# Moving activations, whole weight slabs and block sums to another distance, modulo 512 bytes, from the weight ring

## The chip, the cores and the metric

The kernel runs on one core of one Trainium2 chip. The metric is the device time of one execution in microseconds (us); lower is better. One execution is also recorded by the hardware profiler, and all rows below are of that one. TensorE is called PE in the rows, its weight loads PEld, VectorE DVE, ScalarE ACT and GpSimd POOL. SP issues most of the transfers from memory.

## The reference

One decoder layer, 512 tokens by 2048 channels, all in float32. Cut to what matters:

```
proj = x @ w_in                      # 2048 -> 4180, split among four head groups
mix  = concat(pool(..), conv(..), sparse_attention(..), nsa_attention(..))
x    = layernorm(alpha * x + mix @ w_out)             # 2048 -> 2048
gate, up = split(x @ w_gate_up)                       # 2048 -> 2 * 5632
x    = layernorm(alpha * x + (silu(gate) * up) @ w_down)   # 5632 -> 2048
```

The three large matrix products (w_in, w_out, and the feed-forward pair w_gate_up and w_down) hold most of the work, the feed-forward part by far the most.

## The kernel before

**Every product is three matmuls.** A float32 operand is split into a high part (rounded to the format float32r) and a low part (what is left). A product is high times high, high times low and low times high, each a matmul instruction of its own with its own load of 128 weight columns: the *stationary* operand is loaded into the array, the *moving* operand streams past it. L799 to L801 are the three in the input projection and in the first slabs of the feed-forward part, L1034 to L1036 those of the output projection, L1152, L1154 and L1156 those of gate and up, L1201, L1203 and L1205 those of down.

**The feed-forward part** uses a seven-product scheme on blocks of 2 by 2 (Strassen's form). A chunk makes 128 columns of gate and up for all 512 tokens by seven products; one product is 8 steps of three matmuls, 24 in all, each with 128 weight columns stationary and 256 tokens moving. There are 42 chunks of this kind. Their seven products, numbered 0 to 6 by the second argument of `product`, take as moving operand:

- products 0, 5 and 6: quarters of `act`, the split activations themselves;
- product 1: the block sum s1, which lies in `xs_1` in the room `x_room`;
- product 2: s2, in `xs_2`, in `x_room` as well;
- product 3: s4, in `xs_4`, a room of its own (in the rows `xs`);
- product 4: s3, which was written over a quarter of `act`.

The weights of all seven come from the *ring*: four places for a high part and four for a low one in `w_room`, each of 1024 words per partition. After every four chunks two units of down follow, with the blocks of the hidden layer (`h`, `hs`) stationary and the ring moving, 512 columns wide.

**Whole slabs** of 2048 words are what the stages ahead of the chunks use: two in `w_room` too, laid over the ring but starting `SHIFT` words later, and for a few slabs at the seam between output projection and feed-forward two in `x_room` (`spare_1`, `spare_2`) and one in `xs_4` (`spare_4`).

**Who feeds PE.** SP loads weights into `raw` and `raw_c`; ACT writes the high part into the ring (L1490), DVE the low part (L2041) and the differences of weight blocks (L2049 to L2056). All of this order is written out by hand, with semaphores; there is no scheduler. PE waits for `lo_ready` ahead of each product.

**Where things lie.** The distances within a partition follow from the sizes in the code. All rooms but a few have sizes that are multiples of 512 bytes, so only the start modulo 512 matters for what is told here. Counted from the start of the ring, modulo 512 bytes:

| room | before | after |
|---|---|---|
| ring in `w_room` (high and low places) | 0 | 0 |
| whole slabs in `w_room` | 32 | 64 |
| `act`, with s3 in it | 32 | 64 |
| `raw` | 32 | 64 |
| s1 in `xs_1` | 64 | 32 |
| s2 in `xs_2`, s4 in `xs_4`, and the slabs `spare_1`, `spare_2`, `spare_4` | 64 | 64 |
| `h` blocks, `hs`, `raw_c`, the last weights (`late`) in `x_room`, the mixers' tiles in `proj` | 0 | 0 |

Of the kernel before, what the change touches and what calls it, by code (L numbers as in the profile page):

```python
# [21 lines left out]
F32 = mybir.dt.float32  # L22
F32R = mybir.dt.float32r
# [4 lines left out]
P = 128  # L28
# [22 lines left out]
SLAB = 2048  # L51
# [47 lines left out]


GRAN = SLAB // 2
SHIFT = 8
X_SHIFT = 144
HALF_TOKS = SEQ // 2
S_ORDER = ("s1", "s2", "s4", "s3")
TAIL_SLOTS = ((0, 32), (2, 32), (4, 63), (5, 63), (1, 32), (3, 32), (0, 33), (2, 33))
# [36 lines left out]
def build(nc, x, x_t, w_in, w_out, pool_w, pool_scale, conv_w, conv_b, conv_ln_g, conv_ln_b, conv_pw_w,  # L143
          conv_pw_b, cmp_pos_k, cmp_pos_v, cmp_k_w1, cmp_k_w2, cmp_v_w1, cmp_v_w2, ln1_g, ln1_b,
          ln2_g, ln2_b, w_gate_up, w_down, out):
    with ExitStack() as ctx:
        def sb(name, shape, dt=F32, where=ctx):
            return where.enter_context(nc.sbuf_tensor(name, shape, dt))

        def sem(name):  # L150
# [5 lines left out]
        std = sb("std", [P, TT])  # L156
        w_room = sb("w_room", [P, 4 * SLAB + P + SHIFT], F32R)
        w_hi, w_lo = (w_room[:, SHIFT + at:SHIFT + at + 2 * SLAB].rearrange("p (s n) -> p s n", s=2)
                      for at in (0, 2 * SLAB + P))
# [3 lines left out]

        between = sb("between", [P, P - SHIFT])

# [30 lines left out]
        feed = ExitStack()  # L196
# [17 lines left out]
        h23 = sb("h23", [P, 2, 2, SEQ], F32R, feed)  # L214
        a2_scope = ExitStack()
        with a2_scope:
            below_s1 = sb("below_s1", [P, X_SHIFT], F32, a2_scope)
            s1 = sb("s1", [P, KT // 2, HALF_TOKS], F32, a2_scope)
            below_a2 = sb("below_a2", [P, SLAB], F32, a2_scope)
            a21 = sb("a21", [P, KT // 2, HALF_TOKS], F32, a2_scope)  # L220
            a22 = sb("a22", [P, KT // 2, HALF_TOKS], F32, a2_scope)
        x_room = sb("x_room", [P, 4 * SLAB + X_SHIFT], F32R, feed)
        xs_1, xs_2 = (x_room[:, X_SHIFT + at:X_SHIFT + at + 2 * SLAB].rearrange("p (a k n) -> p a k n", a=2, n=HALF_TOKS)
                      for at in (0, 2 * SLAB))
        first_norm = ExitStack()
        with first_norm:
            ln1_gain = sb("ln1_gain", [P, D_MODEL], F32, first_norm)
# [2 lines left out]
        with s4_scope:  # L230
# [20 lines left out]


        spare_1, spare_2 = ((x_room[:, at:at + SLAB], x_room[:, at + SLAB:at + 2 * SLAB])
                            for at in (X_SHIFT, X_SHIFT + 2 * SLAB))
        spare_4 = tuple(xs_4[:, a, :, :].rearrange("p k n -> p (k n)") for a in range(2))
        late = [(x_room[:, at:at + GRAN], x_room[:, at + GRAN:at + 2 * GRAN]) for at in range(0, 8 * GRAN, 2 * GRAN)]

# [2003 lines left out]
```

How the kernel before makes its waits and increments, by code:

```python
        def copied(eng, n):  # L451
            eng.wait_ge(bank_free[n % 2], n // 2 + 1)
# [1 line left out]
        def tile_ready(eng, group, slab, i):  # L455
            if i < TT - 1:
                eng.wait_ge(tile_done, group * (TT - 1) + (i + 1))
            else:
                eng.wait_ge(slab_done, slab + 1)
# [4 lines left out]
        @block.sync  # L465
# [19 lines left out]
            rows = ((conv_w[0], 0, CONV_WIDTH), (conv_b, V_CB, 1), (conv_ln_g, V_LG, 1),  # L485
                    (conv_ln_b, V_LB, 1), (conv_pw_b, V_PB, 1), (pool_scale, V_PS, 1))
            for src, at, n in rows:
                nc.sync.dma_start(sel[at:at + n, 0:SEQ], src).then_inc(small_loaded, 16)
            nc.sync.dma_start(sel[0:CMP_BLOCK, SEQ:SEQ + P], cmp_pos_k[0]).then_inc(small_loaded, 16)
            nc.sync.dma_start(sel[CMP_BLOCK:2 * CMP_BLOCK, SEQ:SEQ + P], cmp_pos_v[0]).then_inc(small_loaded, 16)
            nc.sync.dma_start(w2[:, 0, :], cmp_k_w2[0]).then_inc(small_loaded, 16)
            nc.sync.dma_start(w2[:, 1, :], cmp_v_w2[0]).then_inc(small_loaded, 16)
            for n in (2, 3):
                sp.wait_ge(part_lo, n + 3)
                load(n % 2, win[:, :, C_IQ + n * P:C_IQ + (n + 1) * P], KT)
            sp.wait_ge(split_done, N_IKWG - 1)
            ikwg = raw[:, 0, 0:KT * (W_IKW + W_NG)].rearrange("p (k n) -> p k n", k=KT)
# [2 lines left out]
            with sp.Fori(0, 4) as c:
                sp.wait_ge(split_done, 2 * c + (N_CONV - 1))
                load(1, win[:, :, bass.ds(c * P + C_G, P)], KT)
```

## Time and profile before

| | before |
|---|---|
| median of 3 runs | 1964.51 us (1962.86 to 1965.04) |
| the profiled execution | 1964.08 us |
| its span, first to last instruction | 1962.2 us |
| PE busy, of the span | 99% |
| DVE busy, of the span | 72% |
| ACT busy, of the span | 43% |
| chunks and down units together | from 710.5 us to 1905.9 us of the span |

The profiled execution's own time lies 1.9 us above its span. A busy PE says only that some matmul was under way: matmuls overlap each other in the rows, since one takes some 280 ns from its start to its end while the next starts after less than half of that. How fast PE goes is read from the starts, by dividing the time between two of them by the matmuls that start between.

### The profile page before, as it was taken

The page shows a single profiled execution, that of the slowest core. Times are in us where ns is not written, and L with a number is a line of the kernel's source. Part 1 is how long each engine was busy: PE and PEld are TensorE (multiplying, and loading weights), DVE is VectorE, ACT ScalarE, POOL GpSimd, SP SyncE. Part 2 cuts the span into 40 slices and gives each one's busy share as a digit, 9 for nine tenths or more (in the row PEclk, how much of TensorE's full clock was granted, in tenths as well). Part 3 has the DMA queues.
Part 4 walks back from the last instruction along what each step waited for, and adds up shares of the span by engine and source line. Part 5 has one row for each costly group of instructions (what it writes and reads, how often), then busy time and mean ns, then how long its engine had stood idle before and what let it go on. Part 6 is the DMA issues. An engine that isn't in the chain of part 4 may idle for free.

```text
span 1962.2 us, 30226 instructions
## 1 busy us (share of the span) xinstructions
PE 1952.2 (99%) x12301; PEld 1731.7 (88%) x12301; DVE 1412.2 (72%) x1911; ACT 848.4 (43%) x1280; POOL 504.1 (26%) x343
## 2 busy tenths in 40 slices
PE   9999999999999999999999999999999999999998
PEld 7777888866888999998989999899998989999896
DVE  3079997274112988887878888888788888878777
ACT  3011001265000545556565555655555555555553
POOL 2555656244567310202011020201102020110200
PEclk9999999999999999999999999999999999999999
DMA  7433343500524524938557394754839376493972
GB/s 214 105 89 80 92 103 90 177 21 25 214 86 131 170 65 129 184 118 166 136 130 172 114 187 126 156 149 116 186 98 203 111 158 152 111 200 90 204 244 87
DMA packets 316429, 264.28 MB, mean 135 GB/s; under 512 B 12262, under 2 KB 258854, under 8 KB 313482
## 3 DMA queue, kind: packets, MB, share of 16 engines
q1 hardware_dynamic: 292026, 211.97, 37.7%
q0 software_dynamic: 23616, 46.15, 14.1%
q10 hardware_dynamic: 656, 4.33, 0.6%
q8 instruction: 93, 1.52, 0.3%
q14 instruction: 38, 0.31, 0.1%
HBM read 211.95 MB, written 50.33 MB: 134 GB/s over the span
## 4 chain that ended last, share of the span: by engine, by line
PE 96%; DMA 1%; DVE 1%; ACT 1%; issue 0%; SPq 0%; DVEq 0%
PE psum L1152 14%; PE psum L1156 14%; PE psum L1154 14%; PE psum L799 7%; PE psum L801 7%; PE psum L800 7%; PE psum L1201 6%; PE psum L1203 6%; PE psum L1205 6%; PE psum L1034 3%; PE psum L1035 3%; PE psum L1036 3%; PE psum L1013 1%; PE psum L950 1%; PE psum L941 1%; PE psum L1001 1%
## 5 line engine op out<-in xcount | busy, mean ns | idle before, releaser
L2041 DVE TENSOR_TENSOR w_room<-raw,w_room 128x1024 fp32r<-128x1024 f32 x310 | 379.5, 1224 | 158.9 <-ACT w_room L1490 158.8
L1490 ACT CAST w_room<-raw 128x1024 fp32r<-128x1024 f32 x312 | 329.1, 1055 | 211.3 <-DVE raw L2052 70.3
L769 POOL DMA_DIRECT2D out<-stage x160 | 139.5, 1472 | 1017.5 <-DVE stage L2152 996.8
L1152 PE MATMUL psum<-act,w_room 128*128 128x256 f32 x1344 | 375.7, 280 | 0.0
L1154 PE MATMUL psum<-act,w_room 128*128 128x256 f32 x1344 | 375.4, 279 | 0.0
L1156 PE MATMUL psum<-act,w_room 128*128 128x256 f32 x1344 | 375.3, 279 | 0.0
L1152 PEld LDWEIGHTS psum<-act,w_room 128*128 128x128 f32 x1344 | 252.6, 188 | 0.4
L1154 PEld LDWEIGHTS psum<-act,w_room 128*128 128x128 f32 x1344 | 252.6, 188 | 0.4
L1156 PEld LDWEIGHTS psum<-act,w_room 128*128 128x128 f32 x1344 | 252.8, 188 | 0.0
L799 PE MATMUL psum<-act,w_room 128*128 128x512 f32 (+2 forms) x608 | 231.8, 381 | 1.7 <-DVE act L1716 1.2
L800 PE MATMUL psum<-act,w_room 128*128 128x512 f32 (+2 forms) x608 | 230.0, 378 | 0.0
L801 PE MATMUL psum<-act,w_room 128*128 128x512 f32 (+2 forms) x608 | 229.9, 378 | 0.0
L677 POOL TENSOR_TENSOR w_room<-raw,w_room 128x2048 fp32r<-128x2048 f32 (+1 forms) x45 | 207.4, 4609 | 3.8
L1152 PE MATMUL psum<-x_room,w_room 128*128 128x256 f32 x672 | 185.6, 276 | 0.0
L1156 PE MATMUL psum<-x_room,w_room 128*128 128x256 f32 x672 | 185.5, 276 | 0.0
L1154 PE MATMUL psum<-x_room,w_room 128*128 128x256 f32 x672 | 185.5, 276 | 0.0
L2041 DVE TENSOR_TENSOR w_room<-raw_c,w_room 128x1024 fp32r<-128x1024 f32 x124 | 151.6, 1223 | 46.9 <-ACT w_room L1490 45.1
L674 POOL TENSOR_SCALAR w_room<-raw 128x2048 fp32r<-128x2048 f32 (+1 forms) x45 | 88.9, 1975 | 259.5 <-PE psum L801 136.9
L799 PEld LDWEIGHTS psum<-act,w_room 128*128 128x128 f32 (+1 forms) x608 | 113.8, 187 | 26.9 <-issue 4.4
L800 PEld LDWEIGHTS psum<-act,w_room 128*128 128x128 f32 (+1 forms) x608 | 113.8, 187 | 22.1 <-issue 0.5
L801 PEld LDWEIGHTS psum<-act,w_room 128*128 128x128 f32 (+1 forms) x608 | 113.8, 187 | 22.1
L1490 ACT CAST w_room<-raw_c 128x1024 fp32r<-128x1024 f32 x126 | 132.9, 1055 | 0.0
(303 smaller groups left out, 4121.5 us busy)
## 6 DMA issues: line engine op xcount, KB each, us to landing
raw_c<-in_w_gate_up SPq DMA_DIRECT2D x84, 512.0 KB, 6.6
raw<-in_w_gate_up SPq DMA_DIRECT2D x84, 512.0 KB, 5.8
out<-stage POOLq DMA_DIRECT2D x160, 256.0 KB, 8.2
raw<-in_w_in SPq DMA_DIRECT2D x30, 1024.0 KB, 5.8
raw<-in_w_down SPq DMA_DIRECT2D x46, 512.0 KB, 4.8
raw_c<-in_w_down SPq DMA_DIRECT2D x42, 512.0 KB, 4.4
raw<-in_w_out SPq DMA_DIRECT2D x16, 1024.0 KB, 5.1
acc<-in_x SPq DMA_DIRECT2D x1, 4096.0 KB, 12.5
```

What stands on the lines that cost most here:

```text
L677: nc.gpsimd.tensor_tensor(lo, raw[:, slot, 0:words], hi.bitcast(F32), ALU.subtract)\
L769: nc.gpsimd.dma_start(out_dram[:, tile, n * SEQ:(n + 1) * SEQ], part, accum_op=ALU.add)\
L799: nc.tensor.matmul(out_ap, stat_hi, mov_hi, start=first, stop=False)
L800: nc.tensor.matmul(out_ap, stat_hi, mov_lo, start=False, stop=False)
L801: return nc.tensor.matmul(out_ap, stat_lo, mov_hi, start=False, stop=last)
L1152: nc.tensor.matmul(out_ap, stat_hi[:, cols], mov_hi[:, k, :], start=opens and k == 0, stop=False, skip_group_check=not opens)
L1154: nc.tensor.matmul(out_ap, stat_hi[:, cols], mov_lo[:, k, :], start=False, stop=False, skip_group_check=not opens)
L1156: mm = nc.tensor.matmul(out_ap, stat_lo[:, cols], mov_hi[:, k, :], start=False, stop=k == kh - 1, skip_group_check=not opens)
L1201: nc.tensor.matmul(out_ap[:, i, :], room[:, 0, j, toks], w_h[:, cols], start=opens and j == 0, stop=False, skip_group_check=not opens)
L1203: nc.tensor.matmul(out_ap[:, i, :], room[:, 1, j, toks], w_h[:, cols], start=False, stop=False, skip_group_check=not opens)
L1490: nc.scalar.copy(ring_hi(at), src).then_inc(hi_ready, 1)
L2041: nc.vector.tensor_tensor(lo, src, hi.bitcast(F32), ALU.subtract).then_inc(lo_ready, 1)
```

## The change

Two constants are changed, and the places of three things follow. `SHIFT` grows from 8 words (32 bytes) to 16 (64 bytes): the slabs in `w_room` begin that much behind the ring's start, and `w_room` gets 8 words longer, by which `act` and `raw` behind it move up. `between` gets shorter by the same, so that nothing behind it moves. In `x_room` the 144 words below the sums become 8 below s1 and 16 below s2; xs_1 loses its distance of 576 bytes (64 modulo 512) and gets one of 32. `below_s1` and `below_a2`, which nobody reads, keep the source of s1 on top of its low part. The program has the same instructions in the same order on each of the five engines, before and after; only addresses differ.

```diff
-SHIFT = 8
-X_SHIFT = 144
+SHIFT = 16
+S1_SHIFT = 8
...
-            below_s1 = sb("below_s1", [P, X_SHIFT], F32, a2_scope)
+            below_s1 = sb("below_s1", [P, S1_SHIFT], F32, a2_scope)
             s1 = sb("s1", [P, KT // 2, HALF_TOKS], F32, a2_scope)
-            below_a2 = sb("below_a2", [P, SLAB], F32, a2_scope)
+            below_a2 = sb("below_a2", [P, SLAB + SHIFT - S1_SHIFT], F32, a2_scope)
...
-        x_room = sb("x_room", [P, 4 * SLAB + X_SHIFT], F32R, feed)
-        xs_1, xs_2 = (x_room[:, X_SHIFT + at:X_SHIFT + at + 2 * SLAB].rearrange("p (a k n) -> p a k n", a=2, n=HALF_TOKS)
-                      for at in (0, 2 * SLAB))
+        x_room = sb("x_room", [P, 4 * SLAB + SHIFT], F32R, feed)
+        xs_1, xs_2 = (x_room[:, at:at + 2 * SLAB].rearrange("p (a k n) -> p a k n", a=2, n=HALF_TOKS)
+                      for at in (S1_SHIFT, SHIFT + 2 * SLAB))
...
-                            for at in (X_SHIFT, X_SHIFT + 2 * SLAB))
+                            for at in (SHIFT, SHIFT + 2 * SLAB))
```

## Rows read from the trace of the kernel before

**Rows 1.** The page: span, busy time by engine, the end chain.

```profile
span 1962.2 us, 30226 instructions
PE 1952.2 (99%) x12301; PEld 1731.7 (88%) x12301; DVE 1412.2 (72%) x1911; ACT 848.4 (43%) x1280; POOL 504.1 (26%) x343
PE 96%; DMA 1%; DVE 1%; ACT 1%; issue 0%; SPq 0%; DVEq 0%
```

**Rows 2.** Stretches of the run: busy us and instructions of each engine.

```profile
core 0: us, PE busy (x) PEld busy (x) DVE busy (x) ACT busy (x) POOL busy (x), PEclk, DMA share, GB/s
710.00:1906.00 1196.00, 1196.00 (x8741) 1130.19 (x8740) 985.02 (x1113) 673.10 (x914) 142.22 (x166) 1.00 0.62 149
```

**Rows 3.** PE's timeline at three borders between products of one chunk: start, duration.

```profile
810.19 0.28 PE L1152 MATMUL psum<-x_room,w_room 128*128 128x256 f32 x1
...
818.35 0.28 PE L1152 MATMUL psum<-act,w_room 128*128 128x256 f32 x1
...
829.56 0.28 PE L1152 MATMUL psum<-x_room,w_room 128*128 128x256 f32 x1
```

**Rows 4.** One window per product, PE alone: products 0 to 6.

```profile
807.39:810.19 2.80, 2.80 (x25) 1.00 1.15 158
810.19:812.91 2.72, 2.72 (x26) 1.00 1.06 185
812.91:815.64 2.73, 2.73 (x27) 1.00 1.13 204
815.64:818.36 2.72, 2.72 (x27) 1.00 1.11 220
818.36:821.17 2.81, 2.81 (x27) 1.00 1.16 314
821.17:823.97 2.80, 2.80 (x27) 1.00 1.20 292
823.97:826.77 2.80, 2.80 (x27) 1.00 0.41 101
```

**Rows 5.** PE's timeline, 512-column matmuls: starts at the borders of runs.

```profile
624.55 0.40 PE L1034 MATMUL psum<-x_room,act 128*128 128x512 f32 x1
630.15 0.40 PE L1034 MATMUL psum<-w_room,act 128*128 128x512 f32 x1
...
688.00 0.40 PE L799 MATMUL psum<-act,xs 128*128 128x512 f32 x1
699.19 0.39 PE L799 MATMUL psum<-act,w_room 128*128 128x512 f32 x1
710.08 0.62 PE L1142 MATMUL psum<-act 128*128 128x512 f32 x2
```

**Rows 6.** The first chunk and the start of the second, columns as in Rows 2.

```profile
713.34:721.82 8.48, 8.48 (x74) 8.48 (x73) 8.48 (x9) 5.36 (x8) 0.00 (x0) 1.00 0.32 90
721.82:733.34 11.52, 11.52 (x98) 11.52 (x97) 9.88 (x13) 5.56 (x8) 0.00 (x0) 1.00 0.44 119
733.34:741.50 8.16, 8.16 (x74) 8.16 (x73) 6.60 (x11) 5.22 (x9) 0.00 (x0) 1.00 0.53 151
```

**Rows 7.** DVE's timeline: the low part that product 3 of the same chunk waits for.

```profile
810.80 1.22 DVE L2041 TENSOR_TENSOR w_room<-raw_c,w_room 128x1024 fp32r<-128x1024 f32 x1
```

**Rows 8.** Groups by form on DVE and PE: xcount, busy us, mean ns, idle before.

```profile
L2041 DVE TENSOR_TENSOR w_room<-raw,w_room 128x1024 fp32r<-128x1024 f32 x310 | 379.5, 1224 | 158.9 <-ACT w_room L1490 158.8
L2041 DVE TENSOR_TENSOR w_room<-raw_c,w_room 128x1024 fp32r<-128x1024 f32 x124 | 151.6, 1223 | 46.9 <-ACT w_room L1490 45.1
...
L799 PE MATMUL psum<-act,w_room 128*128 128x512 f32 x528 | 207.2, 392 | 1.7 <-DVE act L1716 1.2 <-ACT proj L1316 0.4
L1034 PE MATMUL psum<-w_room,act 128*128 128x512 f32 x224 | 87.7, 392 | 0.0
L1034 PE MATMUL psum<-x_room,act 128*128 128x512 f32 x32 | 12.7, 398 | 0.0
```

## The prediction

> **What bounds the kernel now.** I read the page first. PE is busy in 99% of the span and holds 96% of the chain that ended last; DVE, the next engine, is at 72% [rows 1]. So only what makes PE's matmuls fewer or quicker can move the end, and the change leaves their number and order alone. The second view is the table of windows. The chunks and down units take 1196 us, 61% of the span, with PE busy throughout and DVE in 985 us, or 82% [rows 2]. In that stretch nothing makes PE wait, so its time is the sum of its own matmuls' spacings. A busy PE hides how quick it is, so the third view is PE's timeline, read for starts. At 810.19 product 1 of a chunk begins, at 818.35 product 4, at 829.56 product 1 of the chunk behind [rows 3]. From 810.19 to 818.35 there are products 1, 2 and 3, or 72 matmuls in 8.16 us: 2.72 us a product, 113.3 ns a matmul. From 818.35 to 829.56 there are products 4, 5, 6 and 0, or 96 matmuls in 11.21 us: 2.80 us a product, 116.8 ns a matmul.
>
> The windows, one for each product, show the same [rows 4]: 2.80 (product 0), 2.72, 2.73, 2.72 (1 to 3), 2.81 (4), 2.80, 2.80 (5 and 6), at a granted clock of 1.00 in all. (Their counts are 25 to 27, not 24: up to three matmuls from ahead of a border are still ending behind it.) All seven have one shape, 128 weight columns and 256 tokens, their weights come from the same ring, and no engine is waited for. They differ in where the moving operand lies: at 64 bytes from the ring, modulo 512, for the three at 2.72, at 32 for the four at 2.80. The transfers are no explanation: products 5 and 6 take the same 2.80 us, with a DMA share of 1.20 and of 0.41.
>
> A fourth view says whether place matters elsewhere. Matmuls of 512 columns with slabs outside `w_room` are slower as well [rows 5]. From 624.55 to 630.15 there are two tiles of 12 with a slab of `x_room` (at 64) moving and `act` (at 32) stationary: 5.60 us, or 233.3 ns each. From 688.00 to 699.19 the 48 of a slab with `xs_4` (at 64) stationary and `act` moving take 11.19 us, 233.1 ns each. From 699.19 to 710.08 the 48 with slab and `act` both at 32 take 10.89 us, 226.9 ns each.
>
> I choose to read all this as one thing: the spacing depends on the distance of moving and stationary operand modulo 512. At 512 columns a distance of 0 gives 227 ns and 32 either way 233; at 256 columns 32 gives 116.8 and 64 gives 113.3.
>
> At this point a rule of the Trainium skill stands against the change. "TensorE: Matmul & The Clock Gate" (Part 2, Step-by-step: what each phase is for) says that moving operand and weight load have an SBUF read port each, so that loading the next weights takes nothing from the running matmul. By that rule the distance wouldn't matter and the sum below would be 0, where by the rows it is 11 us. The trace disagrees: 2.72 against 2.80 us for products alike in all but place [rows 4].
>
> **The change part by part.**
>
> *Products 0, 4, 5 and 6 go from 32 to 64.* Four products of 11.21 us together [rows 3] become four of 2.72, or 10.88: 0.33 us less for each chunk. All 42 chunks: 13.9 us less. This is the mean over chunks in the steady state; the first is different (below).
>
> *Product 1 goes from 64 to 32.* From 2.72 to the 2.80 of product 0 [rows 4]: 0.08 us more, for 42 chunks 3.4 us more. No row has `xs_1` at 32, so the bounds are nothing (it stays at 2.72) and 0.09 us (as product 4, 2.81), 0 to 3.8 us. I take 3.4, since products 0, 5 and 6 agree.
>
> *Slabs in the spare rooms.* `act` comes to 64, where `spare_1`, `spare_2` and `spare_4` lie: distance 0 in place of 32. L1034 has 32 matmuls of that form [rows 8], its two sister lines as many: 96, four times the 24 of rows 5, each time 5.60 less 5.44 (half of 10.89), 0.16 us: 0.6 us less. The slab of `xs_4`: 11.19 less 10.89, 0.3 us less. Together 0.9 us.
>
> *Slabs in `w_room` with `act`* (projections, the first slabs of the feed-forward part): both move by 32, distance 0 as before. No change, if it is the distance that counts.
>
> *Down, the tail, attention:* `h`, ring, `late` and `proj` stay. No change.
>
> *DVE and ACT* read `raw` at 64 now. DVE's L2041 takes 1224 ns from `raw` (at 32) and 1223 from `raw_c` (at 0) [rows 8], so place costs it nothing; I take the same for ACT.
>
> *Is there room for a quicker PE?* A chunk would last 0.25 us less of 19.4. The low part for product 3 of the chunk read above is begun at 810.80 and done 1.22 us later, at 812.02 [rows 7]; the product starts at 815.64 [rows 4]: 3.6 us of slack. DVE's 82% would become 83%. The work that hides behind PE stays hidden.
>
> Sum: 13.9 − 3.4 + 0.9 = 11.4 us less. The profiled execution took 1964.08 us, 0.4 below the median of the runs, 1964.51. So 1952.7 for it, and about 1953.1 for a median. With only starts at two decimals the 0.33 is good to some 0.02, or 0.8 us over all chunks: the case's own range is 1950.5 to 1955.
>
> **The rivals.**
>
> *A. Product 1 stays quick,* since what makes `act` slow is something other than distance 32 (its rows are 2048 bytes apart, those of the sums 1024), and place at 64 still helps `act`. Then the 3.4 us don't come: 1949.7. Against it: 512-column matmuls from a slab of `x_room`, packed as tightly as the sums, are slow at a distance of 32.
>
> *B. Place doesn't matter at all;* the 0.08 us belong to the rows of `act` being 2048 bytes apart. Then only noise is left: 1964.5, no change. For it: the quick three are just those not in `act`. Against it: the same rows of `act` as stationary operand take 5.60 us with one slab and 5.44 with another [rows 5]. The rule that the Trainium skill gives in "TensorE: Matmul & The Clock Gate", quoted above, would lead to this case as well.
>
> *C. At 512 columns the place 64 itself is slow,* not the distance. Rows 5 can't exclude it: both groups at 233 ns have one operand at 64. Then the chunks gain 10.5, the spare slabs nothing, but all slabs with `act` become as slow as the spare ones: 528 and 224 matmuls on one line each [rows 8], times three lines, 2256, at 0.16 us for 24: 15.0 us more. Sum +4.5: 1969, slower. Against it: nothing but the down products and the ring, which go at 227 at place 0, as slabs do at 32, so that place alone has shown no effect between these two. It decides from some 1,600 of these matmuls on.
>
> *D. A second rhythm of PE.* In the first chunk products 1 to 3 take 8.48 us (2.83 each) and products 4 to 6 with product 0 of the second 11.52 (2.88 each); from 733.34 products 1 to 3 take 8.16 again [rows 6]. Nobody is waited for, the clock is 1.00, and the addresses are the same as later. So there is another rhythm, 0.08 to 0.11 us a product slower, that came and went where product 0 gives way to product 1, so where place 32 gives way to 64. If the new places kept PE in it, a chunk would take six times 2.83 and once 2.88, 19.86 us, against 19.38 now (the sum of rows 4): 0.48 more, 20.2 for 42 chunks, less 0.9: 1983, much slower. It cancels the gain from a third of the chunks on (0.25 a chunk gained or 0.48 lost). Against it: it held for 8 products of 294.
>
> **How the numbers follow.** The forecast as told: 0.70. A 0.08, B 0.06, C 0.05, D in most chunks 0.05; D in a part of them, between 1955 and 1962, 0.06. The predicted time is 1952.8, between the two ways to anchor the sum. A range from 1949 to 1960 holds the forecast, A, and most of the part of D: 0.82. A measurement of this kernel can tell some 0.2%, or 4 us, from no change. Faster by more than that (below 1960.6): 0.70 + 0.08 + 0.05 = 0.83. Within it: B and a little of D, 0.07. Slower: C and D, 0.10.
>
> **What the profile of the changed kernel would show.** In a chunk behind the second, product 1 in 2.80 us and all others in 2.72, the chunk in 19.13; the mean duration of the group of chunk matmuls on `act` down to that of the group on `xs`, and that of the group on `x_room` between the two it had and `act` had, as half of it is product 1. The two tiles with a slab of `x_room` in 5.44 us. L799 and L1034 unchanged in spacing: if they are slower by some 6 ns, it is C. Product 1 at 2.72: A. Nothing moved: B. Products at 2.83 far into the chunks: D. Idle time of PE ahead of a product on L2041 would mean that I misjudged the slack. The prediction is wrong if the product's time doesn't follow from the distance modulo 512 alone.

## The result, and the profile after

The changed kernel takes 1977.2 us (median of 4 runs, 1975.84 to 1979.32), the kernel before 1964.78 beside it: a ratio of 1.0067, with an interval of 1.0051 to 1.0082. Between the medians it is 12.4 us slower, where I had forecast 11.4 us less. Its profiled execution took 1975.84 us, with a span of 1974.0.

The page after, the rows that answer to [rows 1]:

```profile
span 1974.0 us, 30226 instructions
PE 1964.6 (100%) x12301; PEld 1745.6 (88%) x12301; DVE 1411.9 (72%) x1911; ACT 845.9 (43%) x1280; POOL 503.8 (26%) x343
```

PE has the same 12301 matmuls and is busy for 12.4 us longer; the other engines' busy times have hardly moved. So the matmuls themselves have come further apart. The windows, one for each product as in [rows 4], of two chunks: first products 0 to 3 of the second chunk, then those of the fifth. The first down units stand behind the third chunk.

```profile
core 0: us, PE busy (x), PEclk, DMA share, GB/s
728.52:731.25 2.73, 2.73 (x27) 1.00 0.00 0
731.25:734.05 2.80, 2.80 (x26) 1.00 0.00 0
734.05:736.78 2.73, 2.73 (x27) 1.00 0.78 239
736.78:739.50 2.72, 2.72 (x27) 1.00 0.75 234
...
824.69:827.52 2.83, 2.83 (x26) 1.00 0.00 0
827.52:830.32 2.80, 2.80 (x27) 1.00 0.30 86
830.32:833.15 2.83, 2.83 (x27) 1.00 0.89 261
833.15:835.97 2.82, 2.82 (x26) 1.00 0.67 194
```

In the second chunk the forecast stands to a hundredth: product 1 at 2.80 us, all others at 2.72 or 2.73. The later chunk has the same addresses and the same instructions, and everything at 64 takes 2.83. I call the two spacings, 113.3 and 117.8 ns a matmul at 64, the two rhythms of PE. All 39 chunks behind the first down unit are like the fifth, and the groups of the chunk matmuls on `act` and on `x_room` now have the same mean duration:

```profile
L1152 PE MATMUL psum<-act,w_room 128*128 128x256 f32 x1344 | 376.0, 280 | 0.0
L1152 PE MATMUL psum<-x_room,w_room 128*128 128x256 f32 x672 | 187.8, 280 | 0.0
```

The switch is seen in the timeline: the last matmul of down at 804.70, and 0.23 us behind it, with no wait between, product 0 of the fourth chunk.

```profile
804.70 0.39 PE L1205 MATMUL psum<-w_room,h 128*128 128x512 f32 x1
804.93 0.28 PE L1152 MATMUL psum<-act,w_room 128*128 128x256 f32 x1
```

Its window, as above:

```profile
804.93:807.76 2.83, 2.83 (x25) 1.00 1.14 148
```

The first chunk goes a third way. Its product 0, at 64, takes 2.83 us, product 1, at 32, takes 2.88, and from product 2 on those at 64 take 2.72. Here are products 1 and 2:

```profile
712.05:714.93 2.88, 2.88 (x27) 1.00 0.02 6
714.93:717.65 2.72, 2.72 (x27) 1.00 0.66 193
```

The slabs in the spare rooms, the rows that answer to [rows 5]:

```profile
624.01 0.39 PE L1034 MATMUL psum<-x_room,act 128*128 128x512 f32 x1
629.45 0.39 PE L1034 MATMUL psum<-w_room,act 128*128 128x512 f32 x1
...
686.98 0.40 PE L799 MATMUL psum<-act,xs 128*128 128x512 f32 x1
697.88 0.39 PE L799 MATMUL psum<-act,w_room 128*128 128x512 f32 x1
```

24 matmuls in 5.44 us (5.60 before) and 48 in 10.90 (11.19 before), as forecast. The account, added up from the starts in both traces: the 39 chunks behind the first down unit take 19.76 us each in place of 19.37, which is 15.1 us more in all. The first three take 57.6 us together in place of 58.7, 1.2 less. The stage ahead of the chunks is over 1.3 us sooner (the matmuls of L1142 start at 708.76, at 710.08 before). The down units between the chunks take 0.2 us more, and what follows the last chunk is some 1 us shorter. Together that is the span's 11.8 us more.

```profile
708.76 0.61 PE L1142 MATMUL psum<-act 128*128 128x512 f32 x2
```

### The profile page after: what moved, and what is told of

Its sections match the earlier page's. It is cut to its first block, busy times and chain, and to the rows that moved or that the text cites. A ratio compares the mean times of both kernels' runs of the same rounds, so it can differ in the third digit from the quotient of the medians.

```text
span 1974.0 us, 30226 instructions
## 1 busy us (share of the span) xinstructions
PE 1964.6 (100%) x12301; PEld 1745.6 (88%) x12301; DVE 1411.9 (72%) x1911; ACT 845.9 (43%) x1280; POOL 503.8 (26%) x343
## 4 chain that ended last, share of the span: by engine, by line
PE 98%; DVE 1%; DMA 0%; ACT 0%; issue 0%; SPq 0%; DVEq 0%
PE psum L1152 14%; PE psum L1156 14%; PE psum L1154 14%; PE psum L799 7%; PE psum L800 7%; PE psum L801 7%; PE psum L1201 6%; PE psum L1205 6%; PE psum L1203 6%; PE psum L1034 3%; PE psum L1035 3%; PE psum L1036 3%; PE psum L1013 1%; PE psum L950 1%; PE psum L941 1%; PE psum L1001 1%
## 5 line engine op out<-in xcount | busy, mean ns | idle before, releaser
L1152 PE MATMUL psum<-x_room,w_room 128*128 128x256 f32 x672 | 187.8, 280 | 0.0
L1156 PE MATMUL psum<-x_room,w_room 128*128 128x256 f32 x672 | 187.7, 279 | 0.0
L1154 PE MATMUL psum<-x_room,w_room 128*128 128x256 f32 x672 | 187.6, 279 | 0.0
## 6 DMA issues: line engine op xcount, KB each, us to landing
acc<-in_x SPq DMA_DIRECT2D x1, 4096.0 KB, 12.4
```

What stands on the lines that cost most here:

```text
L1152: nc.tensor.matmul(out_ap, stat_hi[:, cols], mov_hi[:, k, :], start=opens and k == 0, stop=False, skip_group_check=not opens)
L1154: nc.tensor.matmul(out_ap, stat_hi[:, cols], mov_lo[:, k, :], start=False, stop=False, skip_group_check=not opens)
L1156: mm = nc.tensor.matmul(out_ap, stat_lo[:, cols], mov_hi[:, k, :], start=False, stop=k == kh - 1, skip_group_check=not opens)
```

## The experiments

**Is it PE alone, and what sets the rhythm?** The first kernel leaves out the layer and keeps only PE's access pattern. Its core, shortened and with comments put in, and a part of the list that it goes through twice:

```diff
+for phase in range(2):                    # DVE and ACT at rest, then busy
+    for kind, shift, d, times in plan():
+        ...
+s += [("down", 0, 0, 1), ("sum", 0, d, 3)]      # for each distance d
+s += [("down", 0, 0, 1), ("sum", 0, 32, 1), ("sum", 0, 64, 2)]
+s += [("down", 0, 0, 1), ("sum", 0, 64, 1), ("sum", 0, 32, 1), ("sum", 0, 64, 1)]
+s += [("down", 0, 0, 1), ("kick", 0, kick, 1), ("sum", 0, 64, 2)]   # kick: 32, 64, 128, 256 columns
```

> This kernel leaves out the layer and writes a part of x as its output. PE runs products like those of the chunks (24 matmuls, 128 weight columns from a ring of four places, 256 columns moving) and units like those of down (12 matmuls of 512 columns at distance 0), first with all other engines at rest, then the same list again with DVE and ACT busy. The distance of the moving operand from the ring goes through 0, 16, 32, 48, 64, 80, 96, 112, 128, 192, 256 and 384 bytes, three products each behind one down unit. Theory 1 (a product's time depends on the distance and on a rhythm that is handed on from one product to the next): products at distance 64 right behind a down unit take 2.83 us each, those behind a product at distance 32 take 2.72, with the other engines at rest as well; at 32 about 2.80. Theory 2 (other engines' reads and writes set the rhythm): with the others at rest, 2.72 in both places and 2.83 only in the second half. Theory 3 (distance is nothing, the rows' pitch in act is what counts): all distances alike at 2.72 at a pitch of 1024 bytes, 2.80 at 2048.

Windows, with DVE and ACT at rest: three products each behind a down unit, at 0, 32, 64 and 112; then the row of products 32, 64, 64 and the row 64, 32, 64, each behind a down unit.

```profile
core 0: us, PE busy (x) PEld busy (x) DVE busy (x) ACT busy (x) POOL busy (x), PEclk, DMA share, GB/s
43.22:51.85 8.63, 8.63 (x73) 8.63 (x72) 0.00 (x0) 0.00 (x0) 0.00 (x0) 1.00 0.01 2
65.88:74.28 8.40, 8.40 (x73) 8.40 (x72) 0.00 (x0) 0.00 (x0) 0.00 (x0) 1.00 0.00 0
88.31:96.80 8.49, 8.49 (x74) 8.48 (x73) 0.00 (x0) 0.00 (x0) 0.00 (x0) 1.00 0.01 2
122.33:130.52 8.19, 8.19 (x73) 8.19 (x72) 0.00 (x0) 0.00 (x0) 0.00 (x0) 1.00 0.01 2
178.65:181.45 2.80, 2.80 (x25) 2.79 (x24) 0.00 (x0) 0.00 (x0) 0.00 (x0) 1.00 0.00 0
181.45:184.17 2.72, 2.72 (x26) 2.72 (x25) 0.00 (x0) 0.00 (x0) 0.00 (x0) 1.00 0.02 6
184.17:186.89 2.72, 2.72 (x26) 2.72 (x25) 0.00 (x0) 0.00 (x0) 0.00 (x0) 1.00 0.00 0
189.64:192.47 2.83, 2.83 (x26) 2.83 (x24) 0.00 (x0) 0.00 (x0) 0.00 (x0) 1.00 0.00 0
192.47:195.26 2.79, 2.79 (x26) 2.79 (x25) 0.00 (x0) 0.00 (x0) 0.00 (x0) 1.00 0.00 0
195.26:198.09 2.83, 2.83 (x26) 2.83 (x25) 0.00 (x0) 0.00 (x0) 0.00 (x0) 1.00 0.00 0
```

8.63 us for three products at distance 0, 8.40 at 32, 8.49 at 64, 8.19 at 112. And a product at 64 takes 2.72 behind a down unit and a product at 32, but 2.83 right behind the down unit; there a product at 32 in between takes 2.79 and doesn't bring the other rhythm back. With DVE and ACT busy (2.63 to 2.77 us of each window) the same row has the same times:

```profile
539.93:542.65 2.72, 2.72 (x26) 2.72 (x25) 2.65 (x3) 2.63 (x4) 0.00 (x0) 1.00 0.03 6
...
548.12:550.95 2.83, 2.83 (x26) 2.83 (x24) 2.73 (x4) 2.77 (x3) 0.00 (x0) 1.00 0.00 0
```

So theory 1 is met, and theory 2 falls: no other engine is needed. Theory 3 falls as well: distance counts at one pitch of rows, and products in a room with the pitch of `act` had the same times (2.80 us at 32, 2.83 at 64). A single matmul ahead of the products changes the rhythm, depending on its width: behind 128 columns the second product at 64 takes 2.82, behind 256 columns 2.72. No simple rule of the width shows: here and in the second PE-only kernel (below) 16, 32, 96 and 160 to 256 columns bring 2.72, and 48, 64 and 128 leave 2.83.

```profile
242.85:245.67 2.82, 2.82 (x26) 1.00 0.00 0
...
251.27:253.99 2.72, 2.72 (x26) 1.00 0.02 6
```

**The two halves of the change, each alone.**

```diff
 # changed kernel, all at 64
-S1_SHIFT = 8
+S1_SHIFT = 16
```

> The changed kernel with s1 at 64 as well, so that activations, slabs and all four block sums are at 64. Theory 1 (a rhythm handed on, set behind a down unit by a product at 64): behind the first down unit all seven products take 2.83 us, a chunk 19.8, the whole some 1978 us, as slow as the changed kernel or 1 us slower. Theory 4 (the one block sum at another distance than the rest is what throws the products out of step): all products 2.72 us, a chunk 19.05, the whole about 1950 us.

Measured: 1979.44 us, ratio 1.0079 (1.0062 to 1.0095), with 19.79 us for every chunk.

```diff
 # kernel before, s1 alone at 32 (x_room as in the changed kernel)
-X_SHIFT = 144
+X_SHIFT = 16
+S1_SHIFT = 8
...
-                      for at in (0, 2 * SLAB))
+                      for at in (S1_SHIFT, X_SHIFT + 2 * SLAB))
```

> The kernel before with s1 alone moved from 64 to 32; activations and slabs stay at 32, s2, s4 and the spare slabs at 64. Theory 1: product 0 at 32 sets the rhythm behind each down unit as before, so products 2 and 3 stay at 2.72 us, product 1 goes to 2.80, a chunk lasts 19.46 us and the whole 1968 us, 3.4 more than before. Theory 4 (the odd block sum throws the rhythm): products 2 and 3 go to 2.83 and those in act to 2.88, the whole is above 1980 us.

Measured: 1968.21 us, ratio 1.0018 (1.0009 to 1.0028). Windows of products 0 to 3 of the fifth chunk in this run:

```profile
829.23:832.03 2.80, 2.80 (x26) 1.00 0.01 1
832.03:834.83 2.80, 2.80 (x26) 1.00 0.21 51
834.83:837.55 2.72, 2.72 (x26) 1.00 0.82 235
837.55:840.27 2.72, 2.72 (x26) 1.00 0.72 204
```

Both came out at theory 1's figure, and theory 4 (the odd block sum is at fault) falls twice. The loss belongs to the activations at 64. Moving s1 costs 4 us by itself, with activations at 32, and costs nothing once they are at 64: there the whole takes 1977.2 us with s1 at 32 and 1979.4 with s1 at 64.

**The rhythm changed, the addresses kept.** One matmul is added in the first chunk and in each chunk behind down units, eleven in all. Its result is overwritten by product 0 behind it, and the wait that comes with it is the one that product 0 has anyway.

```diff
+                if m == 0 or m % 4 == 3:
+                    pe.wait_ge(lo_ready, un.q + 1)
+                    nc.tensor.matmul(r1[par], ring_hi(un.q)[:, 0:P], ring_hi(un.q)[:, 0:HALF_TOKS], start=True, stop=True)
                 product(un, 0, r1[par], act_hi[:, 0:kh, early], act_lo[:, 0:kh, early], True)
```

> The changed kernel with one more matmul, 256 columns of the ring itself (distance 0), in front of product 0 in the first chunk and in each chunk behind the down units: 11 in all, 0.11 us each. Its result is overwritten by the product. Theory 1 (the rhythm is handed on, and that matmul alters it as in the first experiment, from 117.8 ns a matmul to 113.4): products 0 and 2 to 6 at 2.72 us, product 1 at 2.80 to 2.82, a chunk 19.14, the whole 1953.5 us, as was predicted for the change at first. Rival (the rhythm follows from the addresses of the chunk and from nothing ahead of it): still 19.76 us a chunk and 1978 us.

Measured: 1953.29 us, ratio 0.9941 (0.9924 to 0.9958). Windows of products 0, 1, 2 and 6 of the fifth chunk:

```profile
825.32:828.04 2.72, 2.72 (x26) 1.00 0.00 0
828.04:830.85 2.81, 2.81 (x26) 1.00 0.12 33
830.85:833.57 2.72, 2.72 (x26) 1.00 0.82 221
841.73:844.45 2.72, 2.72 (x26) 1.00 0.00 0
```

Eleven more matmuls beside 12301 make the changed kernel 24 us faster. The ten behind down units do it. The one ahead of the first chunk doesn't help: with it the first three chunks take 58.2 us, without it 57.6. This settles the cause of the loss: at the same addresses, what a product takes hangs on what ran ahead of it.

> As the run before it, with s1 at 64 too. Theory 1: all seven products 2.72 us, a chunk 19.04, the whole 1950 us. Rival: 19.8 us a chunk and 1979 us.

Measured: 1951.69 us, ratio 0.9935 (0.9918 to 0.9951). 1950 was expected; the rest is in the first three chunks, at 19.79 each. Windows of a whole chunk, the second and the fifth:

```profile
core 0: us, PE busy (x) PEld busy (x) DVE busy (x) ACT busy (x) POOL busy (x), PEclk, DMA share, GB/s
729.37:749.15 19.78, 19.78 (x170) 19.78 (x169) 17.32 (x24) 10.72 (x17) 0.00 (x0) 1.00 0.36 107
826.20:845.24 19.04, 19.04 (x170) 19.04 (x169) 15.29 (x19) 9.87 (x16) 0.00 (x0) 1.00 0.39 111
```

Ahead of the first chunk stand slabs and the two matmuls of L1142, not a down unit, and there 256 columns didn't help. Two other widths there:

```diff
+                    width = 32 if m == 0 else HALF_TOKS
...
+                    width = 128 if m == 0 else HALF_TOKS
```

> Everything at 64 with the extra matmul ahead of the first chunk cut from 256 columns to 32; the ten behind the down units stay at 256. In the run with 256 everywhere, the first three chunks stayed in the second rhythm at 19.79 us and only those behind a down unit took 19.04. Theory 1 (what counts is the rhythm handed on, and ahead of the first chunk another one is handed on than behind a down unit, so another width alters it): the first three chunks 19.04 each, 2.2 us less in all, 1949.5 us. Rival (the first chunk's rhythm has another cause, such as the waits for the block sums): 19.79 as before and 1951.7 us.

> As the run before it, with 128 columns ahead of the first chunk. Theory 1: one of the widths 32 and 128 gives 19.04 us in the first three chunks; behind a down unit with PE alone 32 columns did so and 128 didn't, here it may be the other way round. Rival: 19.79 with both.

Measured: 1950.85 us with 32 columns, ratio 0.9935 (0.9921 to 0.9948), and 1949.69 in the one run with 128. The second chunk stays at 19.78 and 19.79 us in both, so my expectation failed there and the small difference in time to the run before is none of the rhythm's. The last PE-only kernel (below) had nine widths from 16 to 256 columns behind a slab and those two matmuls, and behind each the products at 64 took 2.83 us from the second on, against my expectation of 2.72 behind some. What brings the first chunk into the quick rhythm with everything at 64 stays open.

**Another distance, without the matmul.**

```diff
-SHIFT = 16
-S1_SHIFT = 8
+SHIFT = 28
...
+        both = sb("w_room", [P, end + 2 * KT * SEQ], F32R)
```

The room `both` holds `w_room` and `act`, and the four block sums go to 112 as well.

> The changed kernel with activations, slabs and all four block sums at 112 bytes from the ring, without an extra matmul (act and w_room are made one room for it). In the first experiment products at 112 right behind a down unit took 113.3 ns a matmul where those at 64 took 117.8. Theory 1 with distance 112 free of the second rhythm: all seven products 2.72 us, a chunk 19.04, the whole 1950 us. Rival (at 112 the rhythm depends on what came before as well, and here something else comes before): products above 2.8 us in a part of the chunks, 1960 to 1990 us.

Measured: 1960.96 us, ratio 0.9983 (0.9974 to 0.9993). Windows of a whole chunk, then of two slabs (96 matmuls) of the input projection; the same 96 of the changed kernel stand in a fence of their own.

```profile
835.09:854.13 19.04, 19.04 (x171) 19.04 (x169) 15.28 (x19) 9.87 (x16) 0.00 (x0) 1.00 0.38 111
211.39:233.79 22.40, 22.40 (x98) 18.05 (x97) 21.41 (x31) 1.21 (x3) 13.02 (x5) 1.00 0.37 94
```

```profile
207.10:228.86 21.76, 21.76 (x98) 18.02 (x96) 20.80 (x30) 1.20 (x3) 13.08 (x5) 1.00 0.34 96
```

Both halves of the expectation are met in part: the chunks are at 19.04 us from the first on (19.08 right behind down units), with no extra matmul, but slab and `act`, still at distance 0 from each other, take 233.3 ns a matmul where they took 226.7, and the first chunk starts at 720.76, some 10 us later than before. So here place does count at 512 columns, with the distance unchanged.

> As the first experiment (it leaves out the layer as well), with the distances 56 to 72 and 100 to 124 in steps of 4 bytes, 176, 240 and 368, each behind a down unit; products at 64 and then at 112 behind one product at 0, 16, 32, 48, 96, 112 and 128; and single matmuls of 16 to 256 columns ahead of products at 64. Theory 1, with distances counted modulo 128: 240 and 368 as 112, 113.3 ns a matmul, 176 as 48, 118.3. A product at 64 goes at 113.3 or at 117.8 by what is ahead of it; at 112 at 113.3 always. If distances count modulo 512 only, 240 and 368 differ from 112.

A product at 240 took 2.81 us and one at 368 took 2.72, as at 112:

```profile
194.35:197.16 2.81, 2.81 (x26) 1.00 0.00 0
205.45:208.17 2.72, 2.72 (x26) 1.00 0.00 0
```

The one at 176 took 119.3 ns a matmul where 48 has 118.3. So distances don't repeat after 128 bytes; my expectation was wrong in that. 368 agrees with a period of 256, and so do 0 and 256, and 128 and 384 in the first PE-only kernel, all four at 120.0. At 64 the products went at 113.3 only behind one at 32, and at 117.8 behind 0, 16, 48, 96, 112 and 128; at 112 they went at 113.3 from the second product on in every order tried, and at 113.3 to 115.6 in the first. Distances of 100 to 108 and 116 to 124 were at 118.9 or above.

> As the first experiment (the layer is left out). Runs of 48 matmuls of 512 columns, a slab stationary and the activations moving, both at 0, 16, 32, 48, 64, 80, 96 and 112 bytes from the ring, and some at unequal places; then a slab at 64, two matmuls of the activations with themselves, a single matmul of 0 to 256 columns, and products at distance 64. If at 512 columns only the distance counts, all runs with equal places take 226.7 ns a matmul. If the place counts too, as the kernel with everything at 112 suggests (233.3 ns in the projections), those at 16, 48, 80 and 112 take 233.3 and those at multiples of 32 take 226.7. For the products: 113.3 ns behind some widths and 117.8 behind others.

24 matmuls of 512 columns, slab and activations both at 16, 32 and 112 from the ring:

```profile
63.42:68.94 5.52, 5.52 (x25) 1.00 0.00 0
77.16:82.61 5.45, 5.45 (x26) 1.00 0.00 0
146.02:151.62 5.60, 5.60 (x25) 1.00 0.00 0
```

230.0, 227.1 and 233.3 ns a matmul. At 48 and 80 it was 231.2, at 0, 64 and 96 226.6 to 227.1. Multiples of 32 are free of the cost, as expected. Of the others only 112 has the 233.3 that I expected for all four.

## Why the prediction was wrong

**Distance counts for the spacing of PE's matmuls: right, but it isn't all.** It shows in the second chunk, in the spare slabs, and with PE alone (8.40 us for three products at 32, 8.63 at 0). The prediction called itself wrong if the time didn't follow from the distance modulo 512 alone, and it doesn't.

**Products 0, 4, 5 and 6 from 32 to 64, 13.9 us less: here it failed.** The step took 2.72 us as what a product at 64 takes, "for each chunk", "all 42 chunks". That is what a product at 64 takes in one of the two rhythms. In the other it takes 2.83, more than the 2.80 of a product at 32. Before, the stretch at 64 always began behind product 0 at 32. After, product 0 stands at 64 right behind the down unit, and the PE-only kernel has exactly these two sequences, with 2.72 and 2.83 us. In 39 of 42 chunks the four products gained nothing and lost some 0.1 us together, and products 2 and 3, whose addresses the change doesn't move, lost 0.11 us each. Over all 42 chunks, from the starts in both traces, products 0, 4, 5 and 6 take 473.7 us in place of 471.2: 2.6 us more where the term says 13.9 less. Products 2 and 3 take 236.9 in place of 228.7: 8.2 us more, a term that the sum doesn't have.

**Rival D was the case:** 2.83 us for a product at 64, behind the down units. I gave it 0.05, and 0.06 more for a part of the chunks, and held against it that "it held for 8 products of 294" (by [rows 6] it is seven, products 1 to 6 of the first chunk and product 0 of the second). That count was taken with the old addresses, under which the first product behind a down unit lay at 32; the change took away just that. The prediction put the border of the rhythms where place 32 gives way to 64, and this isn't the rule. The changed chunk still has that passage, from product 1 to product 2, and the PE-only row 64, 32, 64 keeps 2.83. In the kernel before, the first chunk passed from 32 to 64 and went to 2.83 [rows 6]. Where a product at 32 took 2.88 us, the next at 64 took 2.72, in all four traces that have such a pair; behind one of 2.80 both occur. The price of D, 0.48 us a chunk, came out at 0.38, since product 1 at 32 takes 2.80 in these chunks where I had put 2.88.

**Product 1, 3.4 us more: right** in the kernel before (3.96 us between medians of 1968.21 and 1964.25), and 3.2 us between the two traces of the change. **Slabs in the spare rooms, 0.9 us less: right** (0.16 for 24 matmuls, 0.29 for 48). **Slabs in `w_room`, no change: right** (96 matmuls in 21.76 us, 226.7 ns each), so rival C falls for place 64; the run at 112 shows that place by itself can cost at 512 columns. **Slack: right**: with a chunk at 19.04 us nothing waited on DVE's low parts, which is 0.34 us a chunk quicker than before. Rivals A and B fall with the second chunk, where product 1 takes 2.80 us and the products in `act` 2.72.

The rule of two read ports, from the Trainium skill's "TensorE: Matmul & The Clock Gate" (Part 2, Step-by-step: what each phase is for), would have the loads take nothing from the running matmul. It doesn't account for the PE-only rows: the same matmuls with the same loads take 113.3 ns at a distance of 112 and 120.0 at 0.

## What to carry to other kernels

Where weight loads and matmuls follow each other without a gap, a rate read from the trace belongs to an address pattern *and* to what ran just before. Ask of a change not only which operand moves, but which sequences of patterns it removes, and look for stretches where the same instructions at the same addresses go at two rates: they are the warning. A list of such sequences on PE alone is one short kernel, and it has this loss: 2.83 us for products at 64 right behind a down unit. The best version here, all at 64 with one throwaway matmul of 256 columns ahead of the first product behind each down unit (and one of 32 ahead of the first chunk, which brought nothing), takes 1950.85 us, 0.65% less than the kernel before; with 256 columns in all eleven it is 1951.69, the same within the noise.

## What the runs showed of the hardware

PE alone, with 256 moving columns and 128 weight columns each, has two stable spacings at one set of addresses (distance 64), 113.3 and 117.8 ns a matmul, at a granted clock of 1.00. In the layer it keeps either through four chunks, 672 matmuls. Behind a down unit, a single matmul of 256 columns in 0.11 us moves it from the slower to the quicker, one of 128 does not; behind slabs and the two matmuls of L1142 none of nine widths did. Distances 0, 96 and 128 give 120.0 ns, 32 gives 116.7 and 112 gives 113.3; four bytes to either side of 112 it is 120.0 and 121.7. The shift of the whole pattern by 32 or 64 bytes changed nothing in these products.

At 512 columns two spacings at one set of addresses occur too. In the first and in the second PE-only kernel 24 such matmuls at the same addresses (distance 64) took 233.3 and 228.9 ns each, behind others at distances of -32 and -16:

```profile
354.83:360.43 5.60, 5.60 (x25) 1.00 0.00 0
488.25:493.74 5.49, 5.49 (x26) 1.00 0.02 3
```

That the two read streams collide is a guess that fits; no run here looked inside, and what makes the two rhythms stays open.
